# A hybrid MLA and HGRN2 layer with a hierarchical MoE on one Trainium2 core: where ScalarE rounds the first half of a slot's second weights

## The reference

```python
for e in range(N_EXPERTS):
    he = jax.nn.silu(t @ w1[e]) * (t @ w3[e])
    y = y + gates[:, e:e + 1] * (he @ w2[e]).astype(jnp.float32)
```

## Time and profile before

| what | us |
|---|---|
| median of three runs (lowest, highest) | 1196.34 (1193.72, 1200.63) |
| the profiled execution | 1192.97 |
| its span | 1191.2 |
| TensorE matmul busy, share of the span | 1065.0 (89%) |
| TensorE weight load busy | 861.4 (72%) |
| VectorE busy | 697.3 (59%) |
| ScalarE busy | 524.0 (44%) |
| GpSimd busy | 345.4 (29%) |

### The profile page before, as it was taken

One profiled execution on the slowest core, in us unless ns is written; L12 is line 12 of the kernel. 1 busy time (PEld: TensorE's weight loads), 2 busy tenths in 40 slices (PEclk: granted clock), 3 DMA queues, 4 the chain that ended last, 5 costly groups with the idle time before them and its releaser, 6 DMA issues.

```text
span 1191.2 us, 17980 instructions
## 1 busy us (share of the span) xinstructions
PE 1065.0 (89%) x5777; PEld 861.4 (72%) x5777; DVE 697.3 (59%) x1326; ACT 524.0 (44%) x1025; POOL 345.4 (29%) x368
## 2 busy tenths in 40 slices
PE   5999999998987899999999999974999999999950
PEld 4889889984555677777778777763777887888840
DVE  4330610118665767576565655448777777778867
ACT  4432421213542333323333333313787888888823
POOL 3100510000541111111110101201655565656755
PEclk9999999999988999899999999996999999999985
DMA  8340141123579686565655444844888777766677
GB/s 278 115 164 1 45 126 65 45 76 71 192 269 346 225 318 242 182 230 198 205 200 194 162 164 150 298 155 158 290 322 303 267 266 263 283 256 259 254 246 271
DMA packets 88356, 242.82 MB, mean 204 GB/s; under 512 B 14224, under 2 KB 30048, under 8 KB 78048
## 3 DMA queue, kind: packets, MB, share of 16 engines
q0 software_dynamic: 23328, 122.17, 28.9%
q1 hardware_dynamic: 63904, 117.42, 28.0%
q10 hardware_dynamic: 1056, 2.36, 0.6%
HBM read 243.31 MB, written 48.94 MB: 245 GB/s over the span
## 4 chain that ended last, share of the span: by engine, by line
PE 60%; DMA 14%; DVE 9%; issue 7%; ACT 6%; POOL 2%; SPq 0%; POOLq 0%; ACTq 0%; DVEq 0%
DMA below<-in_w 9%; PE ps L1078 5%; PE ps L2195 4%; PE ps L2196 4%; PE ps L2197 4%; PE ps L931 4%; PE ps L949 3%; PE ps L1119 3%; PE ps L1027 3%; PE ps L2190 3%; PE ps L2189 3%; PE ps L2191 3%; PE ps L1120 3%; PE ps L1123 3%; DVE low L1845 2%
## 5 line engine op out<-in xcount | busy, mean ns | idle before, releaser
L1845 DVE TENSOR_TENSOR low<-below,high 128x1024 fp32r<-128x1024 f32 x128 | 156.4, 1260 | 30.0 <-ACT high L1542 24.8
L1641 PE MATMUL ps<-high 128*128 128x512 f32 x384 | 156.8, 408 | 9.0 <-DVE low L1855 5.8
L1517 POOL TENSOR_TENSOR low<-below,high 128x1024 fp32r<-128x1024 f32 x62 | 128.2, 2069 | 89.8 <-ACT high L1562 88.7
L1642 PE MATMUL ps<-low,high 128*128 128x512 f32 x384 | 151.3, 394 | 0.0
L1643 PE MATMUL ps<-high,low 128*128 128x512 f32 x384 | 151.3, 394 | 0.0
L1542 ACT ACTIVATE high<-below 128x1024 fp32r<-128x1024 f32 x128 | 129.9, 1069 | 33.8 <-DMA below<-in_w 33.7
L655 ACT ACTIVATE arena<-ps 128x512 f32<-128x512 f32 (+8 forms) x100 | 50.0, 509 | 171.8 <-PE ps L931 171.4
L931 PE MATMUL ps<-arena 128*128 128x128 f32 (+4 forms) x613 | 93.9, 276 | 8.0 <-ACT arena L655 2.2
L799 POOL DMA_DIRECT2D high<-wo_dram x34 | 18.6, 547 | 282.2 <-PE ps L1123 269.8
L1641 PEld LDWEIGHTS ps<-high 128*128 128x128 f32 x384 | 72.9, 190 | 25.9 <-issue 9.1
L931 PEld LDWEIGHTS ps<-arena 128*128 128x128 f32 (+4 forms) x613 | 71.2, 148 | 25.5 <-issue 18.1
(11 more groups left out here) (251 smaller groups left out, 2215.5 us busy)
## 6 DMA issues: line engine op xcount, KB each, us to landing
below<-in_w SPq DMA_DIRECT2D x128, 512.0 KB
high<-wo_dram POOLq DMA_DIRECT2D x36, 1024.0 KB, 6.0
low<-wo_dram POOLq DMA_DIRECT2D x36, 1024.0 KB, 8.4
below<-in_w POOLq DMA_DIRECT2D x64, 512.0 KB
y_dram<-arena SPq DMA_DIRECT2D x32, 512.0 KB
arena<-in_x_prompt SPq DMA_DIRECT2D x15, 512.0 KB
below<-in_w_in SPq DMA_DIRECT2D x14, 512.0 KB, 7.8
out<-arena SPq DMA_DIRECT2D x9, 512.0 KB, 2.8
```

The lines of the kernel that those rows point to most:

```text
L1517: pool.tensor_tensor(w2_lo[s % UN][:, c], w2_in[:, c], w2_hi[s % UN][:, c].bitcast(F32), ALU.subtract).then_inc(s_w2lo, 1)
L1641: pe.matmul(out, x_hi, w_hi, start=start, stop=False)
L1642: pe.matmul(out, x_hi, w_lo, start=False, stop=False)
L1845: dve.tensor_tensor(chunk(w13_lo[j], c), chunk(w13_in, c), chunk(w13_hi[j], c).bitcast(F32), ALU.subtract).then_inc(s_w13lo, 1)
```

## The change

In every slot but the last the rounding of the first half of the second weights moves from ahead of Silu to behind the copies of the next rows, where the rounding of the second half already stands. The last slot is left as it was. Nothing else differs.

```diff
             if not last:
                 split_weights(s + 1, (j + 1) % UN)
-            split_second(s, j, 0)
             if last:
+                split_second(s, j, 0)
                 split_second(s, j, 1)
             act.wait_ge(s_mh, s + 1)
             if not start:
@@
             act.activation(act_h, ps[:, 3 + j, 0:FF], ACT.Silu).then_inc(s_ms, 1)
             if not last:
                 turned(s + 1)
+                split_second(s, j, 0)
                 split_second(s, j, 1)
```

## The result

The change made the kernel slower: 1211.68 us median of 4 runs (1206.78 to 1214.22), beside 1195.03 (1193.27 to 1200.63) for the kernel before on the same chip, a ratio of 1.0121 with an interval of 1.0084 to 1.0158. The forecast was 1200.2 with a range of 1191 to 1209. The profiled execution took 1212.36 us.

The account below looks back on a forecast made before the run. It took a loop of first-weight loads through ScalarE, VectorE and SP, without TensorE, as the bound. Terms -3.6 + 7.2 + 0.3 = +3.9 us on a median of 1196.3 gave 1200.2 us, range 1191 to 1209.

Parts of the forecast that it names:

- The loop bounds, TensorE only follows: Expert stage: first-weight roundings, VectorE's subtractions and SP's loads set the pace, 19.54 us a pair against TensorE's 18.74.
- The product still follows VectorE's last subtraction: Slots loading first weights: VectorE's product starts right after its four subtractions, so an earlier Silu gains nil.
- -3.6 us for Silu no longer behind a late load: Two slots with late second weights and the stretch after the clock's drop: loop shorter by 1.21 us each, 3 x 1.21.
- five loops at 0.6: The first five of the twelve first-weight load loops, each charged 0.6 us for the later second weights.
- +0.3 in the last slot: Last slot: GpSimd hands over later, product up to 1.2 us later, mostly covered by TensorE's down part; +0.3 us.
- Twelve loops at 0.6 us for the later second weights: Expert stage: second weights' loads, issued 1.21 us later, share DMA engines with first weights; 0.6 us per loop, +7.2 us.
- The third rival: First weights are held behind the second: each loop grows by 1.21 us, +11.2 us in sum, 1207.5 us; chance 0.25.
- The 12 loops' first-weight loads (957.13) do not shift: SP's issue of new first weights keeps its time in all twelve loops, while the second weights' loads shift by 1.21 us.

Follow-up runs that it names:

- the fills: The change with GpSimd's subtraction for the second half replaced by two fills in slots 2 to 23: 1212.71 us, 1.0155; same fills in the kernel before: 1194.59 us.
- The change with short subtractions: The change with GpSimd's subtractions for the second weights cut from 1024 to 64 columns a half from slot 2 on: 1195.06 us, 0.9992.
- the harmless run: The kernel before with one GpSimd fill of an unused row buffer ahead of the second weights' load in slots 0 to 23: 1197.96 us, 1.0012.

## Why the prediction was wrong

Taken one by one, on the profiled executions:

- *The loop bounds, TensorE only follows*: right. In both kernels every pair read here ends with a rounding that waited for its load. An earlier Silu brought nothing (1.001).
- *The product still follows VectorE's last subtraction*: right. At 957.48 and at 966.94 it has no idle time before it. TensorE's longer wait for it (3.0 us became 12.1) follows from the longer pairs, not from the slower subtractions: it stands at 957.95, behind subtractions of normal length, and with the fills, where no subtraction in a pair is slowed, it is 13.9 us.
- *-3.6 us for Silu no longer behind a late load, and five loops at 0.6*: -0.6 in sum, measured +0.3.
- *+0.3 in the last slot*: the stretch behind the last load grew by 1.7.
- *Twelve loops at 0.6 us for the later second weights*: **this step failed.** Seven of them grew by 1.64 us each, 11.5 instead of 4.2, which is also above the 1.21 that I had taken for the most it could be. The load did leave 1.0 us later (6.18; I had said 6.4).

What the runs show in place of the 0.6 us: in the change's order what GpSimd issues late, the second weights' load and the gather behind it, is enough for nearly the whole loss. The change with short subtractions and the change with fills have the same order on ScalarE, VectorE at full speed and SyncE's issues at the same times (7.0, last part 9.77). They differ in GpSimd's list: the second weights' halves leave at 5.1 and 5.8 in the one, at 6.00 and 6.84 in the other, and the gather 1 us later too. The pairs are 19.42 and 20.97. (The fills by themselves cost nothing: 19.31 in the kernel before.) Not every such delay costs as much: with short subtractions and the halves at 6.09 and 6.66 the pair is 19.87. In the old order the cost sets in abruptly: a load at 6.05 is free (1.0012), one at 6.30 costs 0.8 us a pair (1.0060). My reckoning, in which 1.21 us of delay could cost at most 1.21 us, was wrong in kind and not only in the number. The third rival, which charged the whole 1.21 us in every loop, came nearest (1207.5) and is still 4 us short of 1211.68.

A second thing was wrong, the sentence "The 12 loops' first-weight loads (957.13) do not shift". They shift, by 0.64 us for the first part and 1.02 for the last, because GpSimd's second subtraction moved onto VectorE's first. I had shifted GpSimd's 4.18 us by 1.21 and asked who waits for their result, but not what runs beside them. The kernel before hardly shows it: from 860 us on none of VectorE's subtractions takes over 1.43 us, for GpSimd ends at 951.09 + 4.18 = 955.27 when VectorE has just begun (954.95). The start of the stage, where one takes 3.02 us, shows it. The Trainium skill (SBUF — State Buffer, Who interferes with whom) states it: a VectorE instruction with two inputs in SBUF contends with a GpSimd instruction that reads SBUF, not with one that only writes it. The runs agree on both: 1.22 us each beside fills, 2.43 in the changed kernel's pairs beside a subtraction. But it isn't shown that this shift costs the change anything: with the fills it is gone, and the pair stays at 20.97.

How the late issue makes 1.64 us of a pair is settled only in part. Shown is: the order itself costs nothing (0.9992 with the load at 5.1); slower subtractions with load and order as before, together with a later gather, cost about 1.0 us in the undisturbed pairs (1.0076). The times of the packets say where the delay stands. In all of these kernels a pair ends 1.4 to 1.65 us behind the last packet of its first weights (1024 packets of 2 KB, on q1). Means of seven pairs, in us behind T0, for the packet that completes 95% of them and for the last one:

| kernel | 95% | last | pair |
|---|---|---|---|
| before | 17.16 | 17.87 | 19.42 |
| before, load at 6.05 | 17.24 | 17.89 | 19.36 |
| before, load at 6.30 | 17.49 | 18.72 | 20.18 |
| change, short subtractions, load at 5.1 | 17.03 | 17.86 | 19.42 |
| change, short subtractions, load at 5.85 | 17.50 | 18.84 | 20.34 |
| change, short subtractions, load at 6.09 | 17.63 | 18.39 | 19.87 |
| change with fills, load at 6.00 | 17.94 | 19.46 | 20.97 |
| change | 18.38 | 19.49 | 21.06 |

So a good part of the loss is a **tail**: most of the weights are there, and the last few packets come late. In the longest pair with the load at 6.30 (T0 = 973.40) this is the queue 18.8 us behind T0, over 0.4 us:

```profile
DMA packets 5, 0.01 MB, mean 26 GB/s; under 512 B 0, under 2 KB 0, under 8 KB 5
q1 hardware_dynamic: 5, 0.01, 6.6%
```

A share of 6.6% of 16 engines is about one engine: its packets follow one another while the others have almost nothing to do, and ScalarE waits. The run with the load at 5.85, whose pairs fall into two groups, has the same tail: 95% at 17.2 and the last packet at 17.7 in the pair of 19.3 us, 17.7 and 19.7 in one of 21.2.

Why one engine falls behind **stays open**, and so does why, in the change's order, a load at 5.85 gave 20.3 and one at 6.09 gave 19.9, and why the halves at 6.00 and 6.84 cost 0.8 us more there than 6.30 and 6.88 in the old order. The profile doesn't name the DMA engine of a packet. The change with fills also carried less in the microsecond 12 us behind T0 (310 GB/s in the mean of seven pairs, 294 in the change, 394 in the harmless run). Two such microseconds, first the change with fills, then the harmless run:

```profile
DMA packets 120, 0.26 MB, mean 256 GB/s; under 512 B 2, under 2 KB 2, under 8 KB 120
...
q1 hardware_dynamic: 112, 0.23, 76.1%
q0 software_dynamic: 8, 0.03, 7.1%
```

```profile
DMA packets 201, 0.40 MB, mean 395 GB/s; under 512 B 8, under 2 KB 8, under 8 KB 201
...
q1 hardware_dynamic: 201, 0.40, 102.9%
```

## What to carry to other kernels

When a step moves in time, lay its whole stretch over the other engines' timelines and ask what it now runs beside, not only who waits for its end: here 1 us of shift put a GpSimd subtraction on top of a VectorE one and held back a load that nothing in the dependencies ties to it. Don't price a late load by its delay. In one order 0.9 us of delay were free and a quarter of a microsecond more cost 0.8 us a pair; in the other order 0.9 to 1.0 us cost 1.55 in one run and 0.45 in another. It takes runs at two or three delays, in the order that is to be used. If a loop of loads sets the pace, the number to read is when the last packets land and not when they are issued: one pair lost only 0.5 us by a last part issued 4.2 us later, and seven pairs lost 1.55 us each with it issued 0.2 us earlier.

## What the runs showed of the hardware

- VectorE's subtraction of 128x1024 with both inputs in SBUF takes 1.22 us beside a GpSimd fill and up to 2.46 beside a GpSimd subtraction in the changed kernel; in other runs single ones took 3.03 us (each half's load right behind its subtraction) and 3.58 (extra GpSimd subtractions), and four in a row 9.00.
- GpSimd did not issue a load right behind a short instruction: with its subtractions cut to 0.31 us, 1.57 us of issue stood between the last of them and the load, and a 0.96 us fill put in there cost nothing.
- When the second queue's packets start depended on when the other queue's load was issued: in the mean of seven pairs they came 3.1 us behind SyncE's issue in the harmless run (load at 6.05), 2.3 us with that load at 6.30, and 2.6 us with it at 5.15.
- The 16 DMA engines did not end a load together: 95% of the packets were through 0.7 us before the last in the kernel before, 1.1 in the change and 1.5 in the change with fills, and in the stretch shown above one engine's share, 6.6%, was at work.
